# Moving the first attention product, the tanh buffers and the attention schedule around the layer boundary of a two-layer encoder kernel

## The reference

```
for layer in range(2):
    h = rmsnorm(x, norm_w[layer])
    if layer == 0:                      # "even"
        u, g_a, q, k, v, g_b = split(h @ ev_w_in)
        a_out = s5_mixer(u, ...) * silu(g_a)    # ends in: g * sigmoid(g @ w_glu + b_glu), g = gelu(y)
        b_out = swa_mixer(q, k, v, sinks, rel_bias) * silu(g_b)
        mix = concat(a_out, b_out) @ ev_w_out
    else:                               # "odd"
        q, k, v, r, a_lr = split(h @ od_w_in)
        mix = gla_mixer(q, k, v, a_lr, ...) * silu(r) @ od_w_out
    x = x + mix
return rmsnorm(x, final_norm)
```

## Time and profile before

| | us |
|---|---|
| median of 3 runs | 1775.11 (1773.44 to 1775.91) |
| the profiled execution's own time | 1775.91 |
| its span, first to last instruction | 1774.0 |
| PE busy in the span | 1673.1 (94%) |
| DVE, ACT, POOL busy | 859.3, 623.7, 280.4 |
| last product of the even block to first of the odd block | 12.1 |

### The profile page before, as it was taken

How to read it: one execution, slowest core, us unless ns; L and a number is a source line. 1 busy time by engine, 2 the same in 40 slices (tenths; PEclk the granted TensorE clock), 3 DMA queues, 4 the chain that set the end, 5 groups by cost and what they waited for, 6 DMA issues and landing times.

```text
span 1774.0 us, 22631 instructions
## 1 busy us (share of the span) xinstructions
PE 1673.1 (94%) x7910; PEld 1346.8 (76%) x7910; DVE 859.3 (48%) x1695; ACT 623.7 (35%) x1567; POOL 280.4 (16%) x500
## 2 busy tenths in 40 slices
PE   3998888999999869999999999999999999979997
PEld 3776666777777658888867888888888888868886
DVE  4767543466667556453343233343434444344443
ACT  4622232467666544332253122222222332131111
POOL 1865000000000161110000022221222211000000
PEclk9999998999999979999999999999999999989999
DMA  8344444445454676322232333333333332184663
GB/s 218 119 136 150 118 131 123 139 147 152 138 153 138 194 206 204 105 96 95 74 106 101 116 109 113 103 113 110 107 119 105 114 103 86 66 256 148 197 193 107
DMA packets 271817, 235.50 MB, mean 133 GB/s; under 512 B 81657, under 2 KB 224825, under 8 KB 271705
## 3 DMA queue, kind: packets, MB, share of 16 engines
q1 hardware_dynamic: 260408, 232.94, 42.1%
q10 hardware_dynamic: 11296, 1.12, 0.5%
HBM read 140.09 MB, written 93.91 MB: 132 GB/s over the span
## 4 chain that ended last, share of the span: by engine, by line
PE 60%; DVE 1%; DMA 1%; SPq 1%; issue 1%; ACT 0%; POOLq 0%; POOL 0%; ACTq 0%; DVEq 0%
PE odd_bank L2127 29%; PE odd_bank L2282 10%; PE odd_bank L2171 9%; PE odd_bank L2152 2%; PE odd_bank L2229 2%; PE odd_bank L2226 1%; PE odd_bank L2227 1%; PE odd_bank L2208 1%; PE odd_bank L2196 1%; PE odd_bank L2185 1%; DVE glu_g_lo L1972 0%; PE odd_bank L2210 0%; PE odd_bank L2136 0%; PE odd_bank L2237 0%; PE odd_bank L2236 0%
## 5 line engine op out<-in xcount | busy, mean ns | idle before, releaser
L2127 PE MATMUL odd_bank<-ht_hi,odd_w_hi 128*128 128x512 f32 x768 | 319.9, 416 | 1.1 <-DVE odd_w_lo L1889 1.1
L2127 PE MATMUL odd_bank<-ht_lo,odd_w_hi 128*128 128x512 f32 x768 | 300.5, 391 | 0.0
L2127 PE MATMUL odd_bank<-ht_hi,odd_w_lo 128*128 128x512 f32 x768 | 299.0, 389 | 0.0
L1185 PE MATMUL ev_acc<-ht_hi,ev_w_hi 128*128 128x512 f32 x576 | 242.5, 421 | 1.5 <-DVE ht_lo L891 1.5
L1185 PE MATMUL ev_acc<-ht_hi,ev_w_lo 128*128 128x512 f32 x576 | 228.7, 397 | 0.0
L1185 PE MATMUL ev_acc<-ht_lo,ev_w_hi 128*128 128x512 f32 x576 | 228.3, 396 | 0.0
L1901 DVE COPY odd_stage<-odd_bank 128x512 f32<-128x512 f32 x96 | 66.4, 691 | 228.2 <-PE odd_bank L2127 228.2
L2127 PEld LDWEIGHTS odd_bank<-ht_hi,odd_w_hi 128*128 128x128 f32 x768 | 144.4, 188 | 40.3 <-issue 7.6
L2127 PEld LDWEIGHTS odd_bank<-ht_lo,odd_w_hi 128*128 128x128 f32 x768 | 144.1, 188 | 32.0
L2127 PEld LDWEIGHTS odd_bank<-ht_hi,odd_w_lo 128*128 128x128 f32 x768 | 144.7, 188 | 27.1
L1185 PEld LDWEIGHTS ev_acc<-ht_hi,ev_w_hi 128*128 128x128 f32 x576 | 110.3, 192 | 30.6 <-issue 4.5
(11 more groups left out here) (286 smaller groups left out, 2943.4 us busy)
## 6 DMA issues: line engine op xcount, KB each, us to landing
odd_gl_in<-scr_heads SPq DMA_DIRECT2D x32, 640.0 KB, 4.2
scr_heads<-odd_stage SPq DMA_DIRECT2D x64, 256.0 KB, 2.0
odd_w_raw<-od_w_in SPq DMA_DIRECT2D x48, 256.0 KB, 3.6
ev_w_raw<-ev_w_in SPq DMA_DIRECT2D x36, 256.0 KB, 4.6
ev_x_tile<-x SPq DMA_DIRECT2D x16, 512.0 KB, 3.8
ev_s_cos_sin<-scr_s_cos_sin SPq DMA_DIRECT2D x32, 256.0 KB
odd_xo_sum<-x SPq DMA_DIRECT2D x16, 512.0 KB, 4.3
scr_x<-odd_xo_sum SPq DMA_DIRECT2D x16, 512.0 KB, 2.8
```

Of the source, the lines that this page charges most:

```text
L1185: mm = pe.matmul(acc[n % 3][:], w[j][:, k, :], h[:, k, t], start=(k == 0 and r == 0), stop=(k == KT - 1 and r == 2))
L2127: mm = pe.matmul(acc[n % 4][:], w[j][:, k, :], h[:, k, t], start=(k == 0 and q == 0), stop=(k == KT - 1 and q == 2))
```

## The change

It has five parts.

1. Order of the accumulations: groups 8 and 9 are no longer taken by halves. The load of group 9's weights and their split go by the same rule as the other groups' (two and four p later than before).
2. A0 goes from 38 to 40: every step of the attention is four p later. The last `turn_v`, the last two `turn_p` and the last two `values` now stand behind the last product (`values` of the last chunk at p = 146), and the last `store_o` at p = 147, behind `load_g(1)` in SP's list. `load_qkv` waits for one semaphore instead of four.
3. SP's list near the end of the even block: load_gate(0), load_gate(1), load_att, load_g(0) at p = 138, 139, 140, 141. Before it was load_gate(0), load_g(0), load_gate(1), load_att at 137, 140, 141, 142. The two ACT copies of g's high part go from p = 142, 143 to 145, 146.
4. The product of attention and gate for block 0 goes from POOL's list in the odd block (between gate_g(2) and gate_g(3)) to the front of its list at the end of the even block, ahead of gate_g(0). Its splits go from i = 11 and 12 to i = 1 (ACT) and i = 3 (DVE).
5. `th` goes from three PSUM banks to two SBUF buffers, and `mixed` writes its result over `raw_lo` instead of over `th`; `tanh_of(i)` waits for mixed(i-2) instead of lower_mix(i-3). So `mixed` and `lower_mix` have both inputs in SBUF, where before one of them was in PSUM. The buffers lie where the first rows of x for the residual land, so `load_xo` waits for the last `mixed`; PE's second output product no longer waits for the last `lower_mix`.

```diff
@@ even_layer
-    accs += in_turn(2, 8) + by_halves(8) + in_turn(10, 16) + by_halves(16)
+    accs = [(g, b) for b in range(NB) for g in range(2)] + [(g, b) for g in range(2, 16) for b in range(NB)]
+    accs += [(16, 0), (16, 1), (17, 0), (17, 1), (16, 2), (16, 3), (17, 2), (17, 3)]
-    A0 = 38
-    LOAD_W = {8 * (g - 1) - 2 * (g in (9, 17)): g for g in range(3, N_GRP)}
-    SPLIT_W = {8 * (g - 1) + 4 - 4 * (g in (9, 17)): g for g in range(3, N_GRP)}
+    A0 = 40
+    LOAD_W = {8 * (g - 1) - 2 * (g == 17): g for g in range(3, N_GRP)}
+    SPLIT_W = {8 * (g - 1) + 4 - 4 * (g == 17): g for g in range(3, N_GRP)}
-                    for k in range(4):
-                        sp.wait_ge(stored[k], 16 * ((accs.index((G_Q + 3, b)) - k) // 4 - 3))
+                    sp.wait_ge(stored[b], 16 * (last_of[G_Q + 3] // 4 - 3))
@@ SP, even block
-                        load_gate(0)
+                    if p in (138, 139):
+                        load_gate(p - 138)
                     if p == 140:
+                        load_att()
+                    if p == 141:
                         load_g(0)
-                    if p == 141:
-                        load_gate(1)
-                    if p == 142:
-                        load_att()
@@ POOL, even block
+                pool.wait_ge(glu.att_in[0], 32)
+                one, two_ = glu.raw_lo[:, 4:8, cols(0)], glu.raw_hi[:, 4:8, cols(0)]
+                g.tensor_tensor(one, one, two_, ALU.mult).then_inc(glu.am_done, 1)
                 pool.wait_ge(glu.g_in[0], 64)
@@ ACT, even block
-                    if p in (142, 143):
-                        h = p - 142
+                    if p in (145, 146):
+                        h = p - 145
@@ gates_output_odd
+        th = [at(f"glu_tanh{j}", 44 + 2 * j, [P, BLK]) for j in range(2)]
-        glu_acc, th = bank[0:3], [bank[3], bank[6], bank[7]]
+        glu_acc = bank[0:3]
-                        sp.wait_ge(glu_full, 12)
+                        sp.wait_ge(mixf_done, N_GLU)
@@ POOL, odd block
-                gate_g(1)
-                gate_g(2)
-                gate_att(0)
-                gate_g(3)
+                for b in range(1, NB):
+                    gate_g(b)
@@ ACT, odd block
-                    if i >= 3:
-                        act.wait_ge(mix_lo_done, i - 2)
-                    s.activation(by_step(th[i % 3][:]), ...)
+                    if i >= 2:
+                        act.wait_ge(mixf_done, i - 1)
+                    s.activation(by_step(th[i % 2][:]), ...)
-                    s.copy(ht_hi[:, q, cols(b)], th[i % 3][:]).then_inc(mix_hi_done, 1)
+                    s.copy(ht_hi[:, q, cols(b)], raw_lo[:, q, cols(b)]).then_inc(mix_hi_done, 1)
-                    if i == 11:
+                    if i == 1:
                         upper_att(0)
@@ DVE, odd block
-                    t = th[i % 3][:]
-                    v.scalar_tensor_tensor(t, t, 1.0, raw_lo[:, q, cols(b)], ALU.add, ALU.mult)
+                    gg = raw_lo[:, q, cols(b)]
+                    v.scalar_tensor_tensor(gg, th[i % 2][:], 1.0, gg, ALU.add, ALU.mult)
-                    v.tensor_tensor(ht_lo[:, q, cols(b)], th[i % 3][:], ht_hi[..], ALU.subtract)
+                    v.tensor_tensor(ht_lo[:, q, cols(b)], raw_lo[:, q, cols(b)], ht_hi[..], ALU.subtract)
-                    if i == 12:
+                    if i == 3:
                         lower_att(0)
@@ PE, odd block
-                    if m == 1:
-                        pe.wait_ge(mix_lo_done, N_GLU)
-                            pe.wait_ge(mix_lo_done, N_GLU)
+                            pe.wait_ge(tanh_glu, N_GLU)
```

More of the change, by code:

```diff
@@ L177, in even_layer @@
 def even_layer(nc, prm, scr, ht_hi, ht_lo, cst, base, glu):
-    accs = [(g, b) for b in range(NB) for g in range(2)]
-    in_turn = lambda g0, g1: [(g, b) for g in range(g0, g1) for b in range(NB)]
-    by_halves = lambda g0: [(g, b) for h in range(2) for g in (g0, g0 + 1) for b in (2 * h, 2 * h + 1)]
-    accs += in_turn(2, 8) + by_halves(8) + in_turn(10, 16) + by_halves(16)
+    accs = [(g, b) for b in range(NB) for g in range(2)] + [(g, b) for g in range(2, 16) for b in range(NB)]
+    accs += [(16, 0), (16, 1), (17, 0), (17, 1), (16, 2), (16, 3), (17, 2), (17, 3)]
     n_acc = len(accs)
@@ L191, in even_layer @@
     S_IN, S_OUT = (lambda s: 40 + 3 * s), (lambda s: 43 + 3 * s)
[L192 to L194 removed]
+    A0 = 40
+    LOAD_W = {8 * (g - 1) - 2 * (g == 17): g for g in range(3, N_GRP)}
+    SPLIT_W = {8 * (g - 1) + 4 - 4 * (g == 17): g for g in range(3, N_GRP)}
     NCH = SEQ // CHUNK
[L196 removed]
+    p_end = 2 * (A0 + NCH + 2)
     stream_at = lambda p, base: (p - base) // 3 if (p - base) % 3 == 0 and 0 <= (p - base) // 3 < NGRP else None
@@ L1720, in tanh_of @@
                     act.wait_ge(glu_full, i + 1)
-                    if i >= 3:
-                        act.wait_ge(mix_lo_done, i - 2)
-                    s.activation(by_step(th[i % 3][:]), in_steps(glu_acc[i % 3][:]), ACT.Tanh, bias=glu_b[:, i % 4:i % 4 + 1], scale=0.25
+                    if i >= 2:
+                        act.wait_ge(mixf_done, i - 1)
+                    s.activation(by_step(th[i % 2][:]), in_steps(glu_acc[i % 3][:]), ACT.Tanh, bias=glu_b[:, i % 4:i % 4 + 1], scale=0.25
                                  ).then_inc(tanh_glu, 1)
@@ L1978, in mixed @@
                     dve.wait_ge(gg_done, i + 1)
-                    t = th[i % 3][:]
-                    v.scalar_tensor_tensor(t, t, 1.0, raw_lo[:, q, cols(b)], ALU.add, ALU.mult).then_inc(mixf_done, 1)
+                    gg = raw_lo[:, q, cols(b)]
+                    v.scalar_tensor_tensor(gg, th[i % 2][:], 1.0, gg, ALU.add, ALU.mult).then_inc(mixf_done, 1)
                 def lower_mix(i):
@@ L1984, in lower_mix @@
                     dve.wait_ge(mix_hi_done, i + 1)
-                    v.tensor_tensor(ht_lo[:, q, cols(b)], th[i % 3][:], ht_hi.ap().bitcast(F32)[:, q, cols(b)],
+                    v.tensor_tensor(ht_lo[:, q, cols(b)], raw_lo[:, q, cols(b)], ht_hi.ap().bitcast(F32)[:, q, cols(b)],
                                     ALU.subtract).then_inc(mix_lo_done, 1)
```

1 line of the change is left out of this document (removed).

## The result

The changed kernel is slower: median 1782.63 us (1782.27 to 1786.44, 5 runs) against 1775.11 (1770.64 to 1776.35, 5 runs of the kernel before), ratio 1.0053, 95% interval 1.0036 to 1.0070. The forecast was 1780.7 us and "slower". The profiled execution took 1782.41 us, its span is 1780.5, so 6.5 us over the span before; the forecast for this difference was 5.6. The sum is near, but its parts are not all those of the forecast, and in part it is near by luck, as the experiments show.

What follows compares the result with a forecast made beforehand. PE, busy 94% of the span, was taken as the bound, so only its work or idle time counts. Boundary +3.8 and GLU stage +1.8 gave +5.6 us on a median of 1775.11: 1780.7 us, range 1773.5 to 1788.

Steps and rivals of the forecast that it cites:

- Slower: Whole kernel: a time above 1778.7 us, given a chance of 0.63.
- I cost them at 0 there: Even block: order of groups 8 and 9, A0 and load_qkv only move work while PE is busy; 0 us.
- The boundary: Between the blocks: chunk 31's chain meets POOL, the last store follows load_g(1); first DMA at 631.7 against 627.94, +3.8 us.
- 3 x 1.55: Boundary: three DVE steps of chunk 31 each wait for one POOL product of 1.55 us, so `sums` end at 620.1.
- The GLU stage: Odd block: DVE instructions with two SBUF inputs take turns with POOL, so block 2 starts at 33.7 against 32.0; +1.8 us.
- 14.1 as before: Start of the GLU stage: PE's first four products end 14.1 us after the block's start, unchanged.
- calls itself wrong if gate_g(3) ends first: GLU stage: a stated sign that the prediction is wrong, gate_g(3) on POOL ending before `lower_g(2)` on DVE.
- the forecast's turns: GLU stage: 5.0 us of DVE and 6.2 of POOL's gate_g(3) run one at a time, from 22.5 to 33.7.
- th in SBUF itself: GLU stage: 512 columns from SBUF take 0.68 us, the time of `lower_mix` from PSUM; 0 us.
- POOL out of DVE's way: Rival, GLU stage: gate_g(3) is through before `lower_g(2)`, saving 7.3 us; 1766.8 us, chance 0.12.
- Starved: Rival, boundary and GLU stage: DVE is held through whole POOL runs, +9 and +5.3; 1789.4 us, chance 0.13.
- The boundary does not get longer: Rival, boundary: DVE meets POOL once, not three times; +0.7 there and +1.8 in GLU, 1777.6 us, chance 0.25.

Runs made afterwards that it cites:

- e6_att_in_odd: The changed kernel with the product of attention and gate and its splits back in the odd block, loads as changed: 1784.61 us against 1771.72 for the kernel before.
- r_before: The kernel before, run again unchanged on another chip: 1770.56 us against 1769.13, ratio 1.0002.
- e3_th_psum: The changed kernel with `th` back in three PSUM banks and `mixed` writing over it: 1774.29 us against 1768.84 for the kernel before.
- e2_by_halves: The changed kernel with groups 8 and 9 by halves again, their weight loads and load_qkv's waits as before, A0 still 40: 1777.10 us against 1768.84 for the kernel before.
- e10_both_undone: The changed kernel with groups 8 and 9 by halves and `th` in PSUM again: 1768.46 us against 1769.34 for the kernel before, ratio 0.9987.
- e8_late_att: The kernel before with POOL's two added waits, load_att issued in the odd block ahead of load_g(3), its product last: 1769.82 us against 1769.13 for the kernel before.

## Why the prediction was right, and where it was not

**Slower: right**, with 6.5 us in the profiled pair against 5.6 forecast; by medians it is 7.5 us on this chip and 15.5 on the second. By its terms: the last product ended 3.4 us later than forecast (617.1 against 613.7); from there to the next block's first DMA it took 16.4 us where the forecast has 18.0; the GLU stage cost 1.1 against 1.8.

That the sum came out within 1 us is in part luck. The profiled execution of before, from which it was worked out, was slow in two stages. Over the profiles, "even" is 617.8 us on average with the order of the change and 613.5 with that of before, and the boundary 17.1 against 13.0: 8.4 us together up to the first GLU product, where the forecast has 3.8.

**"I cost them at 0 there", the order of groups 8 and 9 with A0: this step failed.** The argument looked at PE's cover and at PE's work, and an edge of "about 1 us" was given. It did not walk through SP's list, where a store and the load that waits for it, which move by the same four p, change their order against a stream that comes every third p. The cost is 5.4 us of idle time and 2.3 of slower clock, found in all seven executions with that order (4.97 to 5.56 us of hole) and in neither of the two with the order undone. The five with the order of before have a small wait for `u` of their own, 0.7 to 1.3 us at the longest, so against them the cost is about 6.7: 617.8 less 613.5, and the 2.3 us of attention that moved behind the last product. In the difference of the two profiled executions it shows only as +3.4 on the last product, since "even" varies by several us between executions of the same code, and the profile of before was at 615.6 a slow one (five executions with its order: 609.6 to 615.6).

**The boundary: right in kind, somewhat too large.** Load and product came later than forecast. load_att went out at 604.80, but its second half needed 12.7 us to land (forecast 6 to 8). load_g(0) went into the same queue at 606.59 and itself took 12.04 us to issue; that the one delayed the other is likely and not shown. POOL began at 617.99 and not near 609. It still met the chain, at one place, not three. DVE and POOL in the changed kernel:

```profile
616.29 2.29 DVE L1157 TENSOR_TENSOR ht_lo<-ht_lo_raw,ht_hi 128x2048 fp32r<-128x2048 f32 x1
618.49 4.46 DVE L1081 TENSOR_TENSOR ev_at_small<-ev_at_small 128x4 f32<-128x4 f32 x1
```

```profile
617.99 4.94 POOL L646 TENSOR_TENSOR ht_lo_raw<-ht_lo_raw,ht_hi_raw 128x2048 f32<-128x2048 f32 x1 [458.68 <-DMA ht_hi_raw<-scr_gate_b]
```

`sums`, 0.15 us alone (e6_att_in_odd, at 621.49), waited for the whole product of attention and gate: 4.3 us in one piece, where the forecast has 3 x 1.55 = 4.65. Counted from the end of the last product, `sums` end 5.8 us later (forecast 6.4). Then SP did as forecast: the gate's store at 623.77, load_g(1) in 3.30 us (3.7), the last `store_o` at 627.94 with a landing of 4.1 us (5.0), and the first DMA of the next block at 633.52.

**The GLU stage: right in kind, and its size hangs on the base.** The instructions were held as forecast: seven of the 32 beside POOL's two gates, 1.3 to 1.5 us each. The Trainium skill (SBUF — State Buffer, section "Who interferes with whom") has such an instruction blocked until the one that holds the ports has finished, and the 2.0 to 2.17 us above agree with that; the 9.91 us of r_before, past five instructions of POOL, go beyond it. Two steps came out otherwise. PE's first four products, "14.1 as before", took 13.0: behind 6.27 us of idle time PE ran at clock 0.72 from 633.7 to 640, where behind 12.09 us it had 0.50 for 6 us. And `lower_g(1)` was through 13.9 us after the block's start (643.57 and 3.84), forecast 17.3, held by one POOL product and with nothing held ahead of it. So PE's wait before block 1 was 0.97 us, where the forecast has near 3, and that before block 2, forecast near 5, came out at 7.95. The second step: the forecast has `lower_g(2)` take turns with gate_g(3), and calls itself wrong if gate_g(3) ends first. It did, at 663.72, and `lower_g(2)` ran from 664.19 at its full speed: what made it late was the row of held instructions ahead of it. Block 2 started 33.1 us after the block's start, forecast 33.7, because that row was about as long as the forecast's turns: a right size from a mechanism that is only half right.

Also, the +1.8 was worked out against a profiled execution that was itself starved: without POOL's added waits the stage took 55.9, 54.6, 50.6, 48.4 and 46.8 with one input in PSUM, and 57.0, 57.0, 57.3, 58.1 and 59.7 with both in SBUF. The undoing measures part 5 better than the pair of profiles: 6.4 us (after to e3_th_psum) and 11.3 (e2_by_halves to e10_both_undone). That "th in SBUF itself" costs nothing was true of an instruction alone, and wrong as a term: what the rows show of its cost is that it can now be held. A base that is starved in some executions and not in others may also be why the change cost 0.82% on the second chip, more than the profiles of the first show.

**The rivals.** "POOL out of DVE's way" did not come about: load_g(3) was there for POOL at 655.39, 21.9 us after the block's start, where the rival needed 19. "Starved" came true in the kernel before, not in the changed one. "The boundary does not get longer": it took 16.9 to 17.2 in all executions with the product in the even block.

Left open: what makes a store of q land in 8 us behind the stream's DMAs; what makes the two engines take turns at one time and DVE wait past several products at another; and whether ACT's slower tanh (below) costs PE anything outside the stretch in which DVE was full.

## What to carry to other kernels

When a step is moved in a hand-made order, read the issuing queue's list around its new place, above all what now stands directly behind a wait: a shift of four steps, common to a store and the load behind it, changed their place against a stream with a period of three. The stream no longer gave the store time to land, and from just ahead of it went with a landing of twice the time. Operands in PSUM took VectorE out of GpSimd's way in every profile here (0.67 to 0.70 us beside it as alone); before moving them to SBUF count how many such instructions run beside GpSimd, not what one costs alone. And take the base from several executions: a stage that is sometimes starved makes a change look cheaper by as much as the base was unlucky.

## What the runs showed of the hardware that was not expected

- ACT's tanh with a stepped output, 128x512 from PSUM, took 662 to 664 ns into PSUM (16 of 16, L1723 of before) and 1174 to 1290 ns into SBUF (16 of 16, L1721 of after). The plain cast of the same size into SBUF took 592 ns on average from PSUM (before) and 643 from SBUF (after). That PSUM is the quicker destination for ScalarE is stated by the Trainium skill (ScalarE: Activation LUTs, section "Step-by-step: what each stage is for"); a factor of nearly two with such a view is what this case adds.
- The time that SP needs to issue the same four DMAs of 1 MB went with what was in flight: 3.1 to 3.3 us with no large load just ahead (633.52, 624.22), 9.28 behind load_att's 2 MB (e8_late_att), 12.04 behind the 2 MB of load_att and the 1 MB of load_gate(1) (606.59 in the changed kernel). Everything in SP's list behind them comes later by as much.
- Stores of one size (the q column blocks, 128x512) landed in 8.0 to 9.6 us when they went out 0.65 us behind the stream's store of g (35 of 35 between 285 and 360 us in the 14 profiles), and in 3.1 to 6.2 us otherwise (105).
- After a hole of 5.4 us in which PE was idle its clock stood at 0.77 over the next 10 us, so this hole cost 2.3 us, some 40%, more than its length.
